# An encoder layer's first twenty microseconds: constants loaded late, transposes in three pairs of banks, four weight loads issued from ScalarE

## The chip, the cores and the metric

The kernel runs on one core of a Trainium2 chip. The metric is the device time of the whole kernel in microseconds (us), lower is better. A core has five engines that run side by side, each through its own instruction stream in order: TensorE (PE, matmuls and transposes), VectorE (DVE), ScalarE (ACT), GpSimd (POOL) and SyncE (SP). SyncE and ScalarE can issue transfers (DMAs) from memory into the core; an engine that issues one does nothing else until the issue instruction is over. Engines meet only through semaphores.

## What is computed

One layer of an encoder over 512 tokens of width 1024, in float32, in three sub-layers. Each normalizes its input, works, normalizes the result and adds it to the residual:

```python
h = swiglu(rmsnorm(x, ffn1_pre_norm), ffn1_w_gate, ffn1_w_up, ffn1_w_down)   # 1024 -> 2816 -> 1024
x = x + 0.5 * rmsnorm(h, ffn1_post_norm)
h = hybrid_mixer(rmsnorm(x, mix_pre_norm), w_in, ..., w_out)                 # attention and a gated recurrence
x = x + rmsnorm(h, mix_post_norm)
h = swiglu(rmsnorm(x, ffn2_pre_norm), ffn2_w_gate, ffn2_w_up, ffn2_w_down)
x = x + 0.5 * rmsnorm(h, ffn2_post_norm)

def swiglu(x, w_gate, w_up, w_down):
    return (silu(x @ w_gate) * (x @ w_up)) @ w_down
```

The change touches only what happens before and during the first few matmuls of the first `swiglu`, and four small constants (`hgrn_lb_fwd`, `hgrn_lb_bwd`, `hgrn_out_norm`, `attn_sink`) that are not needed before the mixer, hundreds of microseconds later.

## The kernel before

**Split operands.** Every product of the layer's matrices is made from three matmuls: each operand is split into a high part (rounded to the type `float32r`) and a low part (what is left). For activations these are `XH` and `XL`, for weights `WH` and `WL`. The three matmuls of lines 832 to 834 are `WH`·`XH`, `WH`·`XL` and `WL`·`XH`.

**Weights.** They come in units of 128 x 1024 elements (512 KB). A unit passes through one of four slots: SyncE issues the load into `raw` (line 334), ScalarE makes `WH` by a rounding copy (`hi`, line 492), GpSimd makes `WL` by a subtraction (`lo`, line 413), and TensorE uses them. For the first feed-forward the units alternate between `w_gate` and `w_up`; a unit of gate or up is loaded as 1024 rows of 512 bytes. `ahead(n)` in ScalarE's stream means "make `WH` up to unit n". The first four units are numbers 0 to 3.

**Activations.** The tokens stand in four chunks `c` of 128. For a chunk, ScalarE squares and sums `X[c]` (`square_x`, line 514) and takes the root (`rms_x`, line 539), VectorE takes the reciprocal and writes the normalized chunk to `YB` in two halves (`normed`, lines 1280 and 1286), TensorE transposes it, four 128 x 128 blocks to a half, into a bank of PSUM (`turn`, line 857), ScalarE copies the bank to `XH` (`split_high`, line 546) and VectorE subtracts to get `XL` (`split_low`, line 1295). PSUM has eight banks, `ps[0]` to `ps[7]`. The row of pre-norm weights is spread over all partitions by two matmuls (line 944) into `ps[6]` and `ps[7]`.

**Order at the beginning.** Each engine's order is the order in which its block is written. SyncE issues the identity matrix (needed by every transpose), then `X[0]`, `X[1]`, unit 0, `X[2]`, unit 1, `X[3]`, units 2 and 3. ScalarE issues five small transfers first, the row of norm weights and the four constants, and then starts on `X`. TensorE turns the constants (`vec_rows`, 17 rows) into columns before the first chunk is turned (line 947), and VectorE copies them out (line 1324) before it normalizes the first chunk. All four chunks are turned through the same two banks, `ps[4]` and `ps[5]`, so each chunk waits until `XL` of the chunk before is done.

**First units.** `first_units` runs the first four units twice, each time for half of the tokens (`part` 0 and 1, 256 columns, 24 matmuls for a unit and part): part 0 needs only chunks 0 and 1. Chunk 2 is turned ahead of unit 0, chunk 3 between unit 0 and unit 1. After that a loop runs two gate and two up units a turn, and TensorE, ScalarE, VectorE and GpSimd follow one another through it.

Of the kernel before, what the change touches and what calls it, by code (L numbers as in the profile page):

```python
# [5 lines left out]
P = 128  # L6
# [3 lines left out]
KD = D // P  # L10
# [5 lines left out]
NH = 4  # L16
# [5 lines left out]
NSLOT = 4  # L22
# [95 lines left out]
def encoder_layer(nc, io, out):  # L118
# [3 lines left out]
    with ctx:  # L122
# [155 lines left out]
        def y_bank(s, c, h):  # L278


            return ps[(4, 2, 6, 4)[c] + h] if s == 2 else ps[(0 if h else 4) + c]
# [8 lines left out]
            return 8 * s + 2 * c + h + 1  # L290

        def turn_bank(s, c, h):
            return y_bank(s, c, h) if s else ps[4 + h]


        def wait_y(e, s, c, h):
# [30 lines left out]
        def _(sp):  # L327
            def load(n, quarter, src):

                if n >= NSLOT:  # L330
                    sp.wait_ge(lo_done, quarter * NSLOT + (n - NSLOT + 1))
                nk = src.shape[1]
                dst = raw[:, n % NSLOT, 0:nk * src.shape[2]].rearrange("p (k f) -> p k f", k=nk)
                sp.dma_start(dst, src).then_inc(raw_full[n % NSLOT], 16)
# [9 lines left out]
            def load_x(c):  # L344
                sp.dma_start(X[:, c, :], io["x"][0, chunk(c), :]).then_inc(x_in[c], 16)

            def norm_weights(to, name):
                sp.dma_start(to[:, :, :], io[name][0].partition_broadcast(P).rearrange("p (h f) -> p h f", h=2)).then_inc(weights_in, 16)

            def load_ffn(s, first):  # L350
                gate, up, down = w_of[s]
                for b in range(NSLOT):
                    load(first + b, 0, (gate, up)[b % 2][:, :, (b // 2) * P:(b // 2 + 1) * P])
                    if s == 1 and b < 2:
                        load_x(2 + b)
                with sp.Fori(0, KF // 2 - 1) as i:
                    for b in range(NSLOT):
                        load(first + NSLOT + b, i, (gate, up)[b % 2][:, :, bass.ds(i * (2 * P) + (2 + b // 2) * P, P)])
                for h in range(2):
                    for u in range(KP):  # L360
                        load(first + N_UP + KP * h + u, 0, down[:, 2 * u:2 * u + 2, h * TOK:(h + 1) * TOK])
                        if (h, u) == (0, KP - 1):
                            sp.wait_ge(h_ready, KF * s)
                            norm_weights(TMP, f"ffn{s}_post_norm")
                            if s == 1:
                                norm_weights(SQ, "mix_pre_norm")

            sp.dma_start(ident[:, :], io["t_square"][:, 0:P]).then_inc(ident_in, 16)
            load_x(0)
            load_x(1)  # L370
            load_ffn(1, FFN1)
            for u, unit in enumerate(MIXU):
                if u == NSLOT:
# [104 lines left out]
        def _(act):  # L478
# [92 lines left out]
                    square_y(2 * f + 1, c, 0)  # L571
                ahead(first + N_UP + N_DOWN - 1)

            row = 0
            act.dma_start(TMP[0:1, :, :], io["ffn1_pre_norm"].rearrange("o (h f) -> o h f", h=2)).then_inc(row_in, 16)
            for name in ("hgrn_lb_fwd", "hgrn_lb_bwd"):
                act.dma_start(vec_rows[row:row + 2 * NH, :], io[name].rearrange("r (h p) -> (r h) p", p=P)).then_inc(const_in, 16)
                row += 2 * NH
            act.dma_start(sink[:, :], io["attn_sink"][0].partition_broadcast(P)).then_inc(const_in, 16)
            act.dma_start(vec_rows[4 * NH:NV, :], io["hgrn_out_norm"]).then_inc(const_in, 16)  # L580
            act.wait_ge(set_up, 1)
            preload(ACT.Sqrt)
            for c in range(2):
# [1 line left out]
                rms_x(0, c)  # L585
            ahead(0)
            split_high(0, 0)
            square_x(0, 2)
            rms_x(0, 2)
            ahead(1)  # L590
            split_high(0, 1)
            square_x(0, 3)
            rms_x(0, 3)
            split_high(0, 2)
            ahead(2)
            split_high(0, 3)
            ahead(3)
            act.wait_ge(lb_max, 1)
            nc.scalar.activation(lbr, lbr, ACT.Exp).then_inc(lb_exp, 1)
            ffn(0, FFN1)  # L600
# [227 lines left out]
        def _(pe):  # L828
# [14 lines left out]
            def turn(s, c):  # L843

                for h in range(2):
                    bank = turn_bank(s, c, h)
                    pe.wait_ge(xhat_ready, half_count(s, c, h))
                    if s == 1:
                        pe.wait_ge(x_ready, half_count(0, c, 1))
                        pe.wait_ge(squared, square_count("y", 1, 1, c))  # L850
                    elif s == 2:
                        pe.wait_ge(x_ready, half_count(1, c, 1))
                        pe.wait_ge(squared, square_count("y", 2, 1, c))
                    elif c:
                        pe.wait_ge(xl_ready, half_count(s, c - 1, h))
                    for j in range(4):
                        mm = nc.tensor.transpose(bank[:, j * P:(j + 1) * P], YB[:, 4 * h + j, chunk(c)], ident[:, :])  # L857
                    mm.then_inc(x_turned, 1)
# [17 lines left out]
            def first_units(f, first):  # L876


                s = 2 * f
                turn(s, 2)  # L880
                for part in range(2):
                    t = slice(part * 2 * P, (part + 1) * 2 * P)
                    for u in range(NSLOT):
                        if not u:
                            pe.wait_ge(xl_ready, half_count(s, 2 * part + 1, 1))
                        if not part:
                            pe.wait_ge(lo_done, first + u + 1)
                            if f and not u:
                                pe.wait_ge(mixl_a, TT)
                        for k in range(KD):  # L890
                            mm = three(ps[u][:, t], (first + u) % NSLOT, k, XH[:, k, t], XL[:, k, t], not k, k == KD - 1)
                        if part:
                            mm.then_inc(unit_used, 1)
                        elif u == f:
                            turn(s, 3)

            def ffn(f, first):

# [38 lines left out]
                if not f:  # L937
                    turn(1, 2)

            pe.wait_ge(ident_in, 16)  # L940
            pe.wait_ge(row_in, 16)
            pe.wait_ge(set_up, 1)
            for h in range(2):
                mm = nc.tensor.matmul(ps[6 + h][:, :], SQ[0:1, 0, 0:P], TMP[0:1, h, :], start=True, stop=True)
            mm.then_inc(row_spread, 1)
            pe.wait_ge(const_in, CONST_IN)
            nc.tensor.transpose(ps[4][:, 0:NV], vec_rows[:, :], ident[0:NV, 0:NV]).then_inc(vecs_turned, 1)
            pe.wait_ge(vecs_taken, 1)
            turn(0, 0)
            turn(0, 1)  # L950
            ffn(0, FFN1)
# [286 lines left out]
        def _(dve):  # L1238
# [81 lines left out]
            nc.vector.memset(ones[:, :], 1.0)  # L1320
            nc.vector.memset(eps[:, :], EPS)
            nc.vector.memset(SQ[0:1, 0, 0:P], 1.0).then_inc(set_up, 1)
            dve.wait_ge(vecs_turned, 1)
            nc.vector.tensor_copy(vecs[:, :], ps[4][:, 0:NV]).then_inc(vecs_taken, 1)
            dve.wait_ge(row_spread, 1)
            normed(0, 0)
            normed(0, 1)
            split_low(0, 0)
            normed(0, 2)
            split_low(0, 1)  # L1330
            normed(0, 3)
            split_low(0, 2)
            split_low(0, 3)
            dve.wait_ge(vecs_taken, 1)
            dve.wait_ge(const_in, CONST_IN)
            nc.vector.tensor_scalar(sink_less[:, :], sink[:, :], -1.0, None, ALU.mult)
# [330 lines left out]
```

## Time and profile before

| | |
|---|---|
| time, median of 3 runs | 1064.55 us (1064.37 to 1065.12) |
| the profiled execution's own time | 1064.92 us |
| its span in the profile | 1063.1 us |
| PE busy | 1046.3 us, 98% |
| DVE, ACT, POOL busy | 425.2, 363.4 and 450.5 us |
| mean granted TensorE clock | 0.999 of full speed |

The span runs from the first to the last instruction that the profiler saw; 1.8 us lie around it. TensorE is busy nearly all the time, so what counts is when its stream of matmuls begins, what else it has to execute, and where it waits.

### The profile page before, as it was taken

The page shows a single profiled execution, that of the slowest core. Times are in us where ns is not written, and L with a number is a line of the kernel's source. Part 1 is how long each engine was busy: PE and PEld are TensorE (multiplying, and loading weights), DVE is VectorE, ACT ScalarE, POOL GpSimd, SP SyncE. Part 2 cuts the span into 40 slices and gives each one's busy share as a digit, 9 for nine tenths or more (in the row PEclk, how much of TensorE's full clock was granted, in tenths as well). Part 3 has the DMA queues.
Part 4 walks back from the last instruction along what each step waited for, and adds up shares of the span by engine and source line. Part 5 has one row for each costly group of instructions (what it writes and reads, how often), then busy time and mean ns, then how long its engine had stood idle before and what let it go on. Part 6 is the DMA issues. An engine that isn't in the chain of part 4 may idle for free.

```text
span 1063.1 us, 13360 instructions
## 1 busy us (share of the span) xinstructions
PE 1046.3 (98%) x5075; PEld 866.8 (82%) x5075; DVE 425.2 (40%) x621; ACT 363.4 (34%) x540; POOL 450.5 (42%) x299
## 2 busy tenths in 40 slices
PE   6999999999999999999999999999999999999997
PEld 5988888888888878888777878898888888888886
DVE  4443443434001160365757576644434343420103
ACT  6322222222112264513656575542222222221211
POOL 3444444444444246863324134135444444444440
PEclk9999999999999999999999999999999999999999
DMA  6333333323433243332010114024323333333212
GB/s 221 99 99 99 99 99 89 99 89 99 138 99 99 80 137 100 80 99 60 21 40 21 41 40 139 10 74 136 99 86 98 92 99 99 99 99 119 98 41 80
DMA packets 136300, 96.00 MB, mean 90 GB/s; under 512 B 11442, under 2 KB 120387, under 8 KB 136260
## 3 DMA queue, kind: packets, MB, share of 16 engines
q1 hardware_dynamic: 136080, 95.43, 29.8%
q8 instruction: 27, 0.44, 0.2%
q14 instruction: 13, 0.11, 0.0%
q10 hardware_dynamic: 180, 0.02, 0.0%
HBM read 93.34 MB, written 2.10 MB: 90 GB/s over the span
## 4 chain that ended last, share of the span: by engine, by line
PE 94%; DVE 3%; ACT 1%; issue 1%; DMA 1%; ACTq 0%; DVEq 0%
PE ps L832 19%; PE ps L834 18%; PE ps L833 18%; PE ps L841 9%; PE ps L840 9%; PE ps L839 9%; PE ps L998 2%; PE ps L1092 2%; PE ps L1032 1%; PE ps L1115 1%; PE ps L857 1%; PE ps L1102 1%; DVE YB L1286 1%; ACT SQX L514 1%; DMA vec_rows<-hgrn_out_norm 1%
## 5 line engine op out<-in xcount | busy, mean ns | idle before, releaser
L413 POOL TENSOR_TENSOR WL<-raw,WH 128x1024 fp32r<-128x1024 f32 x132 | 317.1, 2404 | 424.3 <-ACT WH L492 424.3
L832 PE MATMUL ps<-XH,WH 128*128 128x512 f32 (+1 forms) x944 | 360.8, 382 | 0.1
L834 PE MATMUL ps<-XH,WL 128*128 128x512 f32 (+1 forms) x944 | 354.7, 376 | 0.0
L833 PE MATMUL ps<-XL,WH 128*128 128x512 f32 (+1 forms) x944 | 354.5, 376 | 0.0
L492 ACT ACTIVATE WH<-raw 128x1024 fp32r<-128x1024 f32 x162 | 171.0, 1056 | 324.9 <-PE ps L834 172.5
L832 PEld LDWEIGHTS ps<-XH,WH 128*128 128x128 f32 x944 | 178.4, 189 | 44.4 <-issue 13.7
L834 PEld LDWEIGHTS ps<-XH,WL 128*128 128x128 f32 x944 | 178.2, 189 | 32.5
L833 PEld LDWEIGHTS ps<-XL,WH 128*128 128x128 f32 x944 | 178.4, 189 | 31.9 <-issue 1.2
L839 PE MATMUL ps<-WH,hh 128*128 128x512 f32 x352 | 137.1, 389 | 0.0
L841 PE MATMUL ps<-WL,hh 128*128 128x512 f32 x352 | 137.0, 389 | 0.0
L430 POOL TENSOR_TENSOR WL<-raw,WH 128x256 fp32r<-128x256 f32 x120 | 95.2, 828 | 98.5 <-ACT WH L492 98.3
L840 PE MATMUL ps<-WH,hl 128*128 128x512 f32 x352 | 136.9, 389 | 0.0
L1314 DVE TENSOR_TENSOR hl<-SQ,hh 128x512 f32 x44 | 118.7, 2697 | 5.4
L1310 DVE TENSOR_TENSOR SQ<-ps,TMP 128x512 f32<-128x512 f32 x44 | 30.4, 692 | 169.7 <-PE ps L834 169.7
L1256 DVE TENSOR_TENSOR ps<-ps,TMP 128x512 f32<-128x512 f32 x16 | 11.2, 698 | 204.7 <-ACT SQX L514 204.5
L556 ACT ACTIVATE SQX<-ps 128x512 f32<-128x512 f32 x44 | 26.3, 598 | 190.9 <-PE ps L834 190.9
L840 PEld LDWEIGHTS ps<-WH,hl 128*128 128x128 f32 x352 | 66.1, 188 | 13.8
L839 PEld LDWEIGHTS ps<-WH,hh 128*128 128x128 f32 x352 | 66.1, 188 | 13.7
L841 PEld LDWEIGHTS ps<-WL,hh 128*128 128x128 f32 x352 | 66.1, 188 | 13.6
L1307 DVE TENSOR_TENSOR TMP<-ps,SQX 128x512 f32<-128x512 f32 x44 | 30.4, 691 | 94.1 <-ACT SQX L556 94.1
L440 POOL TENSOR_TENSOR W<-Qh,Fg 128x512 f32<-128x512 f32 x8 | 10.3, 1290 | 52.4 <-ACT Fg L666 52.4
L998 PE MATMUL ps<-W,KM 128*128 128x128 f32 x224 | 30.7, 279 | 0.7 <-ACT KM L656 0.7
(163 smaller groups left out, 881.3 us busy)
## 6 DMA issues: line engine op xcount, KB each, us to landing
raw<-ffn_w_gate SPq DMA_DIRECT2D x44, 512.0 KB, 3.7
raw<-ffn_w_up SPq DMA_DIRECT2D x44, 512.0 KB, 3.7
raw<-ffn_w_down SPq DMA_DIRECT2D x44, 512.0 KB, 3.7
raw<-w_in SPq DMA_DIRECT2D x22, 512.0 KB, 3.7
raw<-w_out SPq DMA_DIRECT2D x8, 512.0 KB, 3.3
X<-x SPq DMA_DIRECT2D x4, 512.0 KB, 6.5
raw<-w_in SPq DMA_DIRECT2D x8, 256.0 KB, 3.2
out<-X SPq DMA_DIRECT2D x8, 256.0 KB, 2.0
```

The lines of the kernel that those rows point to most:

```text
L413: pool.tensor_tensor(low, raw[:, s, :], high.bitcast(fp32), ALU.subtract).then_inc(lo_done, 1)
L430: ins = pool.tensor_tensor(WL[:, s, f], raw[:, s, f], WH[:, s, f].bitcast(fp32), ALU.subtract)
L492: nc.scalar.activation(to, raw[:, s, :], ACT.Copy).then_inc(hi_done, 1)
L832: nc.tensor.matmul(dst, WH[:, s, w], xh, start=first, stop=False)
L833: nc.tensor.matmul(dst, WH[:, s, w], xl, start=False, stop=False)
L834: return nc.tensor.matmul(dst, WL[:, s, w], xh, start=False, stop=last)
L839: nc.tensor.matmul(dst, xh, wh, start=first, stop=False)
L840: nc.tensor.matmul(dst, xl, wh, start=False, stop=False)
L841: return nc.tensor.matmul(dst, xh, wl, start=False, stop=last)
L998: mm = nc.tensor.matmul(sides[:, c], KM[:, (g - 1) % 2, chunk(c)], level_queries(h, g - 1, c), start=True, stop=True)
L1307: nc.vector.tensor_tensor(TMP[:, a, :], ps[2 * a][:, :], SQX[:, a, :], ALU.mult).then_inc(gate_taken, 1)
L1314: nc.vector.tensor_tensor(hl[:, j, :], SQ[:, a, :], hh[:, j, :].bitcast(fp32), ALU.subtract).then_inc(h_ready, 1)
```

## The change

ScalarE now issues only the row of norm weights and then the loads of units 0 to 3. SyncE issues `X[0]`, `X[1]`, the identity, `X[2]`, `X[3]`, and after them the four constants. TensorE turns chunks 0 and 1 right away, chunk 2 between units 1 and 2, chunk 3 between units 2 and 3, and the constants at the head of part 1. The chunks are turned through three pairs of banks (`4,5`, `2,3`, `4,5`, `6,7`), so that only chunk 2 still waits for an earlier chunk's `XL`. ScalarE copies chunks 0 and 1 in one go before it makes `WH` of unit 1; VectorE subtracts chunks 0 and 1 before it normalizes chunk 2.

```diff
--- before.py
+++ after.py
@@ -290,7 +290,7 @@
             return 8 * s + 2 * c + h + 1
 
         def turn_bank(s, c, h):
-            return y_bank(s, c, h) if s else ps[4 + h]
+            return y_bank(s, c, h) if s else ps[(4, 2, 4, 6)[c] + h]
 
 
         def wait_y(e, s, c, h):
@@ -347,12 +347,24 @@
             def norm_weights(to, name):
                 sp.dma_start(to[:, :, :], io[name][0].partition_broadcast(P).rearrange("p (h f) -> p h f", h=2)).then_inc(weights_in, 16)
 
+            def load_constants():
+
+                row = 0
+                for name in ("hgrn_lb_fwd", "hgrn_lb_bwd"):
+                    sp.dma_start(vec_rows[row:row + 2 * NH, :], io[name].rearrange("r (h p) -> (r h) p", p=P)).then_inc(const_in, 16)
+                    row += 2 * NH
+                sp.dma_start(vec_rows[4 * NH:NV, :], io["hgrn_out_norm"]).then_inc(const_in, 16)
+                sp.dma_start(sink[:, :], io["attn_sink"][0].partition_broadcast(P)).then_inc(const_in, 16)
+
             def load_ffn(s, first):
                 gate, up, down = w_of[s]
-                for b in range(NSLOT):
-                    load(first + b, 0, (gate, up)[b % 2][:, :, (b // 2) * P:(b // 2 + 1) * P])
-                    if s == 1 and b < 2:
-                        load_x(2 + b)
+                if s == 1:
+                    load_x(2)
+                    load_x(3)
+                    load_constants()
+                else:
+                    for b in range(NSLOT):
+                        load(first + b, 0, (gate, up)[b % 2][:, :, (b // 2) * P:(b // 2 + 1) * P])
                 with sp.Fori(0, KF // 2 - 1) as i:
                     for b in range(NSLOT):
                         load(first + NSLOT + b, i, (gate, up)[b % 2][:, :, bass.ds(i * (2 * P) + (2 + b // 2) * P, P)])
@@ -365,9 +377,9 @@
                             if s == 1:
                                 norm_weights(SQ, "mix_pre_norm")
 
-            sp.dma_start(ident[:, :], io["t_square"][:, 0:P]).then_inc(ident_in, 16)
             load_x(0)
             load_x(1)
+            sp.dma_start(ident[:, :], io["t_square"][:, 0:P]).then_inc(ident_in, 16)
             load_ffn(1, FFN1)
             for u, unit in enumerate(MIXU):
                 if u == NSLOT:
@@ -571,13 +583,10 @@
                     square_y(2 * f + 1, c, 0)
                 ahead(first + N_UP + N_DOWN - 1)
 
-            row = 0
             act.dma_start(TMP[0:1, :, :], io["ffn1_pre_norm"].rearrange("o (h f) -> o h f", h=2)).then_inc(row_in, 16)
-            for name in ("hgrn_lb_fwd", "hgrn_lb_bwd"):
-                act.dma_start(vec_rows[row:row + 2 * NH, :], io[name].rearrange("r (h p) -> (r h) p", p=P)).then_inc(const_in, 16)
-                row += 2 * NH
-            act.dma_start(sink[:, :], io["attn_sink"][0].partition_broadcast(P)).then_inc(const_in, 16)
-            act.dma_start(vec_rows[4 * NH:NV, :], io["hgrn_out_norm"]).then_inc(const_in, 16)
+            for b in range(NSLOT):
+                src = w_of[1][b % 2][:, :, (b // 2) * P:(b // 2 + 1) * P]
+                act.dma_start(raw[:, b, :].rearrange("p (k f) -> p k f", k=KD), src).then_inc(raw_full[b], 16)
             act.wait_ge(set_up, 1)
             preload(ACT.Sqrt)
             for c in range(2):
@@ -585,16 +594,16 @@
                 rms_x(0, c)
             ahead(0)
             split_high(0, 0)
+            split_high(0, 1)
+            ahead(1)
             square_x(0, 2)
             rms_x(0, 2)
-            ahead(1)
-            split_high(0, 1)
+            ahead(2)
             square_x(0, 3)
             rms_x(0, 3)
+            ahead(3)
             split_high(0, 2)
-            ahead(2)
             split_high(0, 3)
-            ahead(3)
             act.wait_ge(lb_max, 1)
             nc.scalar.activation(lbr, lbr, ACT.Exp).then_inc(lb_exp, 1)
             ffn(0, FFN1)
@@ -851,8 +860,8 @@
                     elif s == 2:
                         pe.wait_ge(x_ready, half_count(1, c, 1))
                         pe.wait_ge(squared, square_count("y", 2, 1, c))
-                    elif c:
-                        pe.wait_ge(xl_ready, half_count(s, c - 1, h))
+                    elif c == 2:
+                        pe.wait_ge(xl_ready, half_count(0, 0, h))
                     for j in range(4):
                         mm = nc.tensor.transpose(bank[:, j * P:(j + 1) * P], YB[:, 4 * h + j, chunk(c)], ident[:, :])
                     mm.then_inc(x_turned, 1)
@@ -877,12 +886,16 @@
 
 
                 s = 2 * f
-                turn(s, 2)
+                if f:
+                    turn(s, 2)
                 for part in range(2):
                     t = slice(part * 2 * P, (part + 1) * 2 * P)
                     for u in range(NSLOT):
                         if not u:
                             pe.wait_ge(xl_ready, half_count(s, 2 * part + 1, 1))
+                            if part and not f:
+                                pe.wait_ge(const_in, CONST_IN)
+                                nc.tensor.transpose(ps[4][:, 0:NV], vec_rows[:, :], ident[0:NV, 0:NV]).then_inc(vecs_turned, 1)
                         if not part:
                             pe.wait_ge(lo_done, first + u + 1)
                             if f and not u:
@@ -891,8 +904,10 @@
                             mm = three(ps[u][:, t], (first + u) % NSLOT, k, XH[:, k, t], XL[:, k, t], not k, k == KD - 1)
                         if part:
                             mm.then_inc(unit_used, 1)
-                        elif u == f:
+                        elif f and u == 1:
                             turn(s, 3)
+                        elif not f and u in (1, 2):
+                            turn(s, 1 + u)
 
             def ffn(f, first):
 
@@ -937,15 +952,12 @@
                 if not f:
                     turn(1, 2)
 
-            pe.wait_ge(ident_in, 16)
             pe.wait_ge(row_in, 16)
             pe.wait_ge(set_up, 1)
             for h in range(2):
                 mm = nc.tensor.matmul(ps[6 + h][:, :], SQ[0:1, 0, 0:P], TMP[0:1, h, :], start=True, stop=True)
             mm.then_inc(row_spread, 1)
-            pe.wait_ge(const_in, CONST_IN)
-            nc.tensor.transpose(ps[4][:, 0:NV], vec_rows[:, :], ident[0:NV, 0:NV]).then_inc(vecs_turned, 1)
-            pe.wait_ge(vecs_taken, 1)
+            pe.wait_ge(ident_in, 16)
             turn(0, 0)
             turn(0, 1)
             ffn(0, FFN1)
@@ -1320,17 +1332,17 @@
             nc.vector.memset(ones[:, :], 1.0)
             nc.vector.memset(eps[:, :], EPS)
             nc.vector.memset(SQ[0:1, 0, 0:P], 1.0).then_inc(set_up, 1)
-            dve.wait_ge(vecs_turned, 1)
-            nc.vector.tensor_copy(vecs[:, :], ps[4][:, 0:NV]).then_inc(vecs_taken, 1)
             dve.wait_ge(row_spread, 1)
             normed(0, 0)
             normed(0, 1)
             split_low(0, 0)
+            split_low(0, 1)
             normed(0, 2)
-            split_low(0, 1)
             normed(0, 3)
             split_low(0, 2)
             split_low(0, 3)
+            dve.wait_ge(vecs_turned, 1)
+            nc.vector.tensor_copy(vecs[:, :], ps[4][:, 0:NV]).then_inc(vecs_taken, 1)
             dve.wait_ge(vecs_taken, 1)
             dve.wait_ge(const_in, CONST_IN)
             nc.vector.tensor_scalar(sink_less[:, :], sink[:, :], -1.0, None, ALU.mult)
```

ScalarE's stream at its beginning, before (names as above; `raw_full0` is the arrival of unit 0, `x_in0` that of `X[0]`):

```order
L575 DMA TMP<-ffn_pre_norm 1x1024
L577 DMA vec_rows<-hgrn_lb_fwd 8x128
L577 DMA vec_rows<-hgrn_lb_bwd 8x128
L579 DMA sink<-attn_sink 128x8
L580 DMA vec_rows<-hgrn_out_norm 1x128
L506 ACT_TABLE_LOAD
L506 ACTIVATE small<-eps 128x1 [waits set_up]
L514 ACTIVATE SQX,stats<-X 128x1024 [waits x_in0]
L539 ACTIVATE stats<-stats,eps 128x1 [waits squared]
```

The same place now:

```order
L586 DMA TMP<-ffn_pre_norm 1x1024
L589 DMA raw<-ffn_w_gate 128x8x128
L589 DMA raw<-ffn_w_up 128x8x128
L589 DMA raw<-ffn_w_gate 128x8x128
L589 DMA raw<-ffn_w_up 128x8x128
L518 ACT_TABLE_LOAD
L518 ACTIVATE small<-eps 128x1 [waits set_up]
L526 ACTIVATE SQX,stats<-X 128x1024 [waits x_in0]
L551 ACTIVATE stats<-stats,eps 128x1 [waits squared]
```

Four small transfers have left ScalarE's stream, and four of 512 KB stand ahead of the table load and the first square.

TensorE's stream from its beginning to the first matmuls of unit 0, before (`ident,YB` are the transposes, eight to a chunk):

```order
L944 MATMUL ps<-TMP,SQ 128x512 x2
L947 MATMUL ps<-ident,vec_rows 128x17
L857 MATMUL ps<-ident,YB 128x128 x24
L832 MATMUL ps<-XH,WH 128x256
L833 MATMUL ps<-XL,WH 128x256
L834 MATMUL ps<-XH,WL 128x256
```

And now, with the place between units 1 and 2 and the one between units 2 and 3:

```order
L958 MATMUL ps<-TMP,SQ 128x512 x2
L866 MATMUL ps<-ident,YB 128x128 x16
...
L866 MATMUL ps<-ident,YB 128x128 x8
L841 MATMUL ps<-XH,WH 128x256
...
L866 MATMUL ps<-ident,YB 128x128 x8
...
L898 MATMUL ps<-ident,vec_rows 128x17
```

Eight transposes (chunk 2) and the turn of the constants have moved from ahead of the first matmul to behind it.

## Rows read from the trace of the kernel before

**Rows 1.** The page's chain that ended last, shares of the span by engine.

```profile
PE 94%; DVE 3%; ACT 1%; issue 1%; DMA 1%; ACTq 0%; DVEq 0%
```

**Rows 2.** Waits of PE after 18.2 us: total, times, longest (us); the longest.

```profile
PE ps L857 <- DVE YB L1286: 0.9, 2, 0.5
```

**Rows 3.** Timeline of ScalarE: start us, us, instruction, [idle before <-releaser].

```profile
2.69 1.28 ACT L506 ACT_TABLE_LOAD   x1 [2.69 <-issue]
5.12 1.06 ACT L514 ACTIVATE SQX<-X 128x1024 f32<-128x1024 f32 x1 [0.94 <-DMA X<-x]
6.30 0.29 ACT L539 ACTIVATE stats<-stats,eps 128x1 f32<-128x1 f32 x1
6.50 1.04 ACT L514 ACTIVATE SQX<-X 128x1024 f32<-128x1024 f32 x1
...
9.75 1.06 ACT L492 ACTIVATE WH<-raw 128x1024 fp32r<-128x1024 f32 x1 [1.79 <-DMA raw<-ffn_w_gate]
11.30 0.60 ACT L546 ACTIVATE XH<-ps 128x512 fp32r<-128x512 f32 x1 [0.49 <-PE ps L857]
```

**Rows 4.** Waits in the first 12 us: the constants.

```profile
PEld ps L947 <- DMA vec_rows<-hgrn_out_norm: 3.8, 1, 3.8
```

**Rows 5.** Timeline of VectorE, 9 to 14 us.

```profile
9.09 0.15 DVE L1280 RECIPROCAL stats<-stats 128x1 f32<-128x1 f32 x1
9.29 1.40 DVE L1286 SCALAR_TENSOR_TENSOR YB<-X,stats,ps 128x512 f32<-128x512 f32 x2
...
10.80 1.40 DVE L1286 SCALAR_TENSOR_TENSOR YB<-X,stats,ps 128x512 f32<-128x512 f32 x2
12.12 1.35 DVE L1295 TENSOR_TENSOR XL<-ps,XH 128x512 fp32r<-128x512 f32 x2
```

**Rows 6.** Timeline of TensorE, 10 to 23 us.

```profile
10.18 1.94 PE L857 MATMUL ps<-ident,YB 128*128 128x128 f32 x8 [1.21 <-DVE YB L1286]
...
16.50 1.94 PE L857 MATMUL ps<-ident,YB 128*128 128x128 f32 x8 [1.61 <-DVE XL L1295]
...
18.09 0.56 PE L832 MATMUL ps<-XH,WH 128*128 128x256 f32 x1
...
22.25 1.04 PE L857 MATMUL ps<-ident,YB 128*128 128x128 f32 x8
```

**Rows 7.** Stretches: length, PE and PEld busy (x instructions), ...; the last numbers are granted clock, DMA share and GB/s.

```profile
18.00:20.70 2.70, 2.70 (x15) 2.70 (x14) 2.23 (x4) 1.76 (x3) 0.61 (x1) 1.00 0.65 191
20.70:31.60 10.90, 10.90 (x93) 10.90 (x93) 4.60 (x10) 5.02 (x7) 4.19 (x2) 1.00 0.33 99
```

**Rows 8.** Timeline of GpSimd: `WL` of unit 0.

```profile
10.89 2.37 POOL L413 TENSOR_TENSOR WL<-raw,WH 128x1024 fp32r<-128x1024 f32 x1 [10.44 <-ACT WH L492]
```

**Rows 9.** Timeline of SyncE's queue: start us, us that the issue took.

```profile
2.20 0.43 SPq L334 DMA_DIRECT2D raw<-ffn_w_gate  x1
2.68 0.58 SPq L345 DMA_DIRECT2D X<-x  x1
3.30 0.48 SPq L334 DMA_DIRECT2D raw<-ffn_w_up  x1
3.82 4.55 SPq L345 DMA_DIRECT2D X<-x  x1
...
8.90 2.15 SPq L334 DMA_DIRECT2D raw<-ffn_w_up  x1
```

**Rows 10.** DMA issues by window: KB each, us to landing; units 0 and 1.

```profile
DMA to landing us min/median/max: 7.5/7.5/7.5
...
raw<-ffn_w_up SPq DMA_DIRECT2D x1, 512.0 KB, 9.2
```

**Rows 11.** Line 334 near 385 us: durations ns, starts; landing; then its next two.

```profile
L334 SPq DMA_DIRECT2D raw<-w_in x2: 432/508/585, 384.9 to 385.4; - x2
...
DMA to landing us min/median/max: 8.0/8.6/9.1
...
L334 SPq DMA_DIRECT2D raw<-w_in x2: 1112/2200/3289, 388.1 to 391.8; - x2
```

**Rows 12.** DMA traffic, 0 to 12 us in 40 slices of 0.3 us.

```profile
GB/s 0 0 0 0 0 26 157 173 109 205 316 355 302 420 328 423 396 369 126 56 2 36 51 85 119 235 306 370 352 393 457 423 394 369 333 326 355 382 408 428
```

## The prediction, made before the change was run

> **What bounds the kernel now.** I read the chain that ended last first: 94% of it is TensorE [rows 1]. Then its waits after 18.2 us: the longest group is 0.9 us in all [rows 2]. So from its first real matmul, at 18.09 us [rows 6], TensorE works without a stop to the end, and the time is the start of that stream plus its length. A microsecond off the start is a microsecond off the kernel, and so is one put on. The profiled span is 1063.1 us in a run of 1064.92; the median is 0.37 us below that run. I add a difference in span straight to the median.
>
> Next, what made the start 18.09. ScalarE's first square began at 5.12, when `X[0]` had landed [rows 3]. Roots were ready soon after (6.30 + 0.29), but TensorE stood 3.8 us for the last constant to land [rows 4], so VectorE took its first reciprocal only at 9.09 [rows 5]. Then the chunks went through one pair of banks: chunk 2's transposes had to wait 1.61 us for `XL` [rows 6], began at 16.50 and, eight in 1.94 us, held up the first matmul. The rebuilt order removes both, the constants' wait and chunk 2's turn, from the path.
>
> **What the change makes of ScalarE.** Call T the moment when ScalarE has issued its fourth weight load. All that follows hangs on T, since table load, squares and roots stand behind it in the same stream. The chain from T, from rows:
> - Table load 1.28 and the little activation behind it: square of chunk 0 starts at T+1.5. From square to root's start 6.30-5.12 = 1.2, root 0.3: root of chunk 0 at T+3.0. Second square 1.4 after the first (6.50-5.12), so the second root ends at T+4.4 [rows 3].
> - VectorE: first reciprocal T+3.05. Before, reciprocal at 9.09, `YB` of chunk 0 at 9.29, of chunk 1 at 10.80 [rows 5], TensorE's eight transposes from 10.18 for 1.94 [rows 6]. Counted from the reciprocal: chunk 0 turned from +1.1 to +3.0; chunk 1's second half of `YB` is there at +3.1, its turn follows without a wait and ends at +5.0, at the same pace.
> - ScalarE copies the last half (0.60 [rows 3]) until +5.65, VectorE subtracts (0.68, half of 1.35 [rows 5]) until +6.35. First matmul at +6.45, which is **T+9.5**.
> - Does unit 0 keep up? Its `WH` is made from T+4.3 to T+5.3 (1.06 [rows 3]), `WL` takes 2.37 [rows 8] until T+7.8. Yes. Unit 1's `WH` comes behind the copies, T+8.7 to T+9.75, `WL` until T+12.2; unit 0's 24 matmuls last some 4 us (2.70 for the first 15, then 0.117 each [rows 7]), until about T+13.5. Units 2 and 3: `WL` at T+14.6 and T+17.1, wanted at T+17.3 and T+20.2 (24 matmuls x 0.12 = 2.9 a unit, 0.9 for a turn). All hidden, with 1.3, 2.7 and 3.1 us to spare. Were one cover gone, its lateness would come on top one for one.
> - The constants' turn, at the head of part 1, costs 0.15 us of TensorE; their transfers have had 20 us to land. ScalarE's exponential waits for them, with two table loads around it, some 3 us beyond the head of part 1; its first gate activation is due 2.9 us beyond, and TensorE asks for its product only after four units, 11.6 us. Hidden.
>
> **What TensorE gets to do behind its first matmul.** Chunk 2's turn is now inside the stream, at the price of chunk 3's there, 1.04 less the overlap at its end: 0.9 us [rows 6]. Constants 0.15. Clock: the granted clock reads 1.00 throughout, but 15 instructions took the first 2.70 us and 93 the next 10.90 [rows 7], 0.18 against 0.117 us each: the first stretch went partly at the lower of the two levels (1.2 GHz against 2.4). Before that TensorE had turned chunks 1 and 2. Now it has a 1.5 us pause between chunk 1's turn and unit 0. I bound the slow stretch at no longer and 1.5 us longer: 0 to 0.5 us, taken as 0.3. Sum: **change = (T + 9.5 - 18.09) + 0.9 + 0.15 + 0.3 = T - 7.2.** Break-even is T = 7.2 us.
>
> **How large is T?** An issue without resistance takes 0.43 to 0.58 us on SyncE's queue [rows 9], and four behind the row would end near 3.1. But SyncE did not get through: with units 0 and 1 issued, `X[3]` was held for 4.55 us, to 8.37, and unit 3 for 2.15 us, to 11.05 [rows 9]. Landings: unit 0 at 2.20 + 7.5 = 9.7, unit 1 at 3.30 + 9.2 = 12.5 [rows 10]. So unit 3 was let in 1.45 us before unit 1 landed. The same pile stands at 385 us: two weight units issued at 384.9 and 385.4 landed at 392.9 and 394.5; the third, tried at 388.1, was in after 3.29 us at 391.4, the fourth, from 391.8 for 1.11, at 392.9 [rows 11]: each 1.5 to 1.6 us before the one two places ahead of it landed. My reading: a queue takes two such units, and a third when the first is almost over. I see this on SyncE's queue only; ScalarE's small issues were never held. If its queue is the same, ScalarE is held at unit 2 and again at unit 3, and **T is about unit 1's landing less 1.5**.
>
> Unit 1 landed at 12.5 behind the identity, `X[0]`, `X[1]`, unit 0 and `X[2]`. Now it is issued at about 1.8, ahead of `X[2]`: one 512 KB transfer less, at some 380 GB/s [rows 12] 1.4 us, gives 11.1 and T = 9.6. That holds if transfers of both queues go in order of issue. If instead `X[2]` and `X[3]`, on the other queue, take their share before unit 1 ends, it lands at 13.9 and T = 12.4. The slump from 5.4 to 7.2 us [rows 12], in which little moved, may go with the small constants out of the way: up to 1.5 us off, T = 8.1. I take T = 10.3, a change of 10.3 - 7.2 = +3.1 us.
>
> The order across queues is where the Trainium skill speaks (DMA: Bandwidth & Descriptors, Queues, rings and completion order): an engine of the DMA hardware takes turns between the queues that have work for it, a packet at a time. By that rule `X[2]` and `X[3]` would share with the weights, and T would be near the upper of the two values, a change of about +5. The constant's late landing speaks rather for order of issue, so the sum stays with its own value.
>
> **Rivals.**
> 1. *ScalarE is not held* (ends faster). Each issue costs 0.43 to 0.58 us and T is 3.1. `X[0]` is issued 0.4 earlier than before and lands at about 4.7 (5.12 less 0.4 [rows 3]), which is as if T were 3.2; the later gate is unit 0, whose `WH` stands ahead of the copies: landed at about 9.7 as before, `WH` to 10.8, four copies at 0.53 to 0.60 to 13.0, `XL` 13.7, first matmul 13.8. Change: 13.8 - 18.09 + 1.35 = -2.9, time 1061.6. It decides when T is below 5.1. For it: five issues on ScalarE's queue were over by 2.69 [rows 3], unhindered. Against: they were of 4 KB and less, and the hold shows at two places wherever a third unit is asked for. Chance 0.15. The Trainium skill states it this way (the same page, Issuing engines are not separate DMA queues): issuing from several engines saves only the sequencer's time, usually small beside the transfer. It names no hold; the rows show one, on SyncE.
> 2. *Only unit 3 is held, and until unit 0 is nearly in*: the limit is three units, as `X[3]`'s release 1.3 us ahead of unit 0's landing could be read. Unit 0 is behind 1 MB of `X` only and lands at 8.5 to 9.7, so T = 7.2 to 8.4, or up to 9.3 with some sharing. Change 0 to +2.1, time about 1065.3. Against: unit 3 and the fourth at 385 us waited longer than this. Chance 0.22.
> 3. *Held as forecast*, T 9.3 to 12.5: +2.1 to +5.3, time 1067.6. Chance 0.57.
> 4. *Worse*: both queues share, and `WL` of a late unit or a longer slow stretch adds: beyond 1069.9. Chance 0.06.
>
> **How the numbers follow.** No change can be told from one of about 0.2%, 2.1 us. Faster is rival 1: 0.15. Slower is cases 3 and 4: 0.63. The rest, 0.22, is rival 2. The likeliest time is 1064.55 + 3.1 = 1067.6; its own range is 1066.6 to 1069.9. The 8-in-10 range runs from 1063.8, which leaves out most of rival 1, to 1070.2.
>
> **What would show it.** Step by step in the new profile: on ScalarE's queue two weight issues of about 0.45 us, then one or two of several microseconds; table load starting near 10 and not at 3; `X[0]` landed long before its square; no wait of TensorE on the constants; first matmul about 9.5 us behind the table load's start, near 20; eight transposes of 0.9 us between units 1 and 2; no new wait later. I am wrong if the issues on ScalarE's queue are all short, if unit 1 lands before 9, or if TensorE waits on `WL` of units 1 to 3.

## The result, and the profile after

| | |
|---|---|
| changed kernel, median of 11 runs | 1067.56 us (1066.6 to 1070.06) |
| kernel before, median of 11 runs | 1064.78 us (1064.32 to 1066.0) |
| ratio | 1.003, 95% interval 1.0021 to 1.0039 |
| profiled execution: its time, its span | 1069.64 us, 1067.8 us |

The change made the kernel slower by 2.8 us, 0.3%. The profiled execution lies 2.1 us above its median, that of before 0.1 us above its own; the two traces therefore differ by more, 4.7 us of span, and a part of that difference needs an explanation of its own.

The chain that ended last is still TensorE's, but the constants' transfer (the 1% of DMA in [rows 1]) has gone from it and ScalarE's issues have come in (ACTq stands for ScalarE's queue):

```profile
PE 93%; DVE 3%; ACT 2%; ACTq 1%; issue 1%; DVEq 0%
```

ScalarE's timeline (start us, us, instruction), the place of [rows 3]:

```profile
1.31 0.41 ACTq L589 DMA_DIRECT2D raw<-ffn_w_gate  x1
1.75 0.59 ACTq L589 DMA_DIRECT2D raw<-ffn_w_up  x1
2.38 4.74 ACTq L589 DMA_DIRECT2D raw<-ffn_w_gate  x1
7.14 4.51 ACTq L589 DMA_DIRECT2D raw<-ffn_w_up  x1
11.69 1.28 ACT L518 ACT_TABLE_LOAD   x1 [11.69 <-issue]
...
13.09 1.04 ACT L526 ACTIVATE SQX<-X 128x1024 f32<-128x1024 f32 x1
...
15.82 1.04 ACT L504 ACTIVATE WH<-raw 128x1024 fp32r<-128x1024 f32 x1
```

Two issues of about half a microsecond, then two of 4.74 and 4.51 us. Nothing else of ScalarE's stream ran meanwhile: the table load starts at 11.69 instead of 2.69, the first square at 13.09 instead of 5.12, without a wait for `X[0]`, which had long landed. T, the moment at which ScalarE is free, is 11.69.

The landings of this kernel's transfers, from its issues by window (KB each, us from issue to landing): units 0 and 1, and `X[3]`, issued at about 2.6:

```profile
raw<-ffn_w_gate ACTq DMA_DIRECT2D x1, 512.0 KB, 10.3
raw<-ffn_w_up ACTq DMA_DIRECT2D x1, 512.0 KB, 11.4
...
X<-x SPq DMA_DIRECT2D x1, 512.0 KB, 7.7
```

Unit 0 landed at 11.6 and unit 1 at 13.15, `X[3]` before both, at 10.3, though it was issued after them. T is 1.5 us ahead of unit 1's landing, as unit 3's issue was in [rows 9, 10] and the fourth in [rows 11]. Unit 2, though, was let in at 7.12, 4.5 us ahead of unit 0's landing.

TensorE's timeline, the place of [rows 6]:

```profile
15.75 3.65 PE L866 MATMUL ps<-ident,YB 128*128 128x128 f32 x16 [9.44 <-DVE YB L1298]
20.81 0.58 PE L841 MATMUL ps<-XH,WH 128*128 128x256 f32 x1 [1.41 <-DVE XL L1307]
...
25.03 0.39 PE L842 MATMUL ps<-XL,WH 128*128 128x256 f32 x1
25.24 0.30 PE L843 MATMUL ps<-XH,WL 128*128 128x256 f32 x1
...
28.62 1.03 PE L866 MATMUL ps<-ident,YB 128*128 128x128 f32 x8
...
36.19 0.23 PE L898 MATMUL ps<-ident,vec_rows 17*128 17x17 f32 x1
```

Chunks 0 and 1 are turned back to back through two pairs of banks, but 5.6 us later than chunk 0 was. The first matmul runs at 20.81, not 18.09. 20 matmuls are slow: up to 25.24 they follow one another by 0.21 us (the first by 0.38), from there by 0.12. Before, 12 were slow, up to 20.80. Chunk 2's turn now stands inside the stream, at 28.62. After it TensorE waits nowhere that it did not wait before: the longest groups of its waits behind the start of the stream are

```profile
PE ps L841 <- DVE XL L1307: 1.4, 1, 1.4
PE ps L866 <- DVE YB L1298: 0.9, 2, 0.5
```

of which the first is the wait ahead of the first matmul itself and the second is that of [rows 2]. The slump in the traffic of [rows 12] is no longer at 5.4 to 7.2 us, but it has moved rather than gone. In the same slices of 0.3 us a shorter one stands at 9.3 to 11.4 us:

```profile
GB/s 0 0 0 0 0 68 191 123 341 410 328 423 341 382 437 393 251 270 316 335 367 382 389 401 425 389 413 393 442 387 366 304 162 111 89 103 180 277 345 341
```

From 9 to 11 us the packets (the pieces in which a transfer moves) were these:

```profile
DMA packets 594, 0.37 MB, mean 186 GB/s; under 512 B 156, under 2 KB 554, under 8 KB 594
```

156 of them were under 512 bytes, against 35 from 6 to 9 us. The only transfer in such small rows is that of the constant `sink` (128 rows of 32 bytes), which SyncE had issued with the others behind `X[3]`, by 4.6 us. So this slump, with the constants in it, lay ahead of the landings of units 0 and 1. What it cost was not tried by itself.

### The profile page after: what moved, and what is told of

Same layout as the page of the kernel before. It is cut to its first block, busy times and chain, and to the rows that moved or that the text cites. A ratio compares the mean times of both kernels' runs of the same rounds, so it can differ in the third digit from the quotient of the medians.

```text
span 1067.8 us, 13357 instructions
## 1 busy us (share of the span) xinstructions
PE 1046.2 (98%) x5075; PEld 867.0 (81%) x5075; DVE 423.5 (40%) x621; ACT 363.3 (34%) x540; POOL 450.1 (42%) x299
## 4 chain that ended last, share of the span: by engine, by line
PE 93%; DVE 3%; ACT 2%; ACTq 1%; issue 1%; DVEq 0%
PE ps L841 19%; PE ps L842 18%; PE ps L843 18%; PE ps L850 9%; PE ps L848 9%; PE ps L849 9%; PE ps L1010 2%; PE ps L1104 2%; PE ps L1044 1%; PE ps L1127 1%; ACTq L589 1%; PE ps L866 1%; PE ps L1114 1%; ACT SQX L526 1%; PE ps L1021 1%
## 5 line engine op out<-in xcount | busy, mean ns | idle before, releaser
L452 POOL TENSOR_TENSOR W<-Qh,Fg 128x512 f32<-128x512 f32 x8 | 10.3, 1290 | 52.5 <-ACT Fg L675 52.5
```

## The experiments

Each ratio is to the kernel before, run on the same chip; its median was 1064.7 to 1065.0 us in these runs. Theory A: ScalarE is held by its own issues, and that alone turns a gain into a loss.

**1. The weight loads back on SyncE's queue, all the rest rebuilt.** The constants thereby come behind the four units.

```diff
# ScalarE
-            for b in range(NSLOT):
-                act.dma_start(raw[:, b, :]..., src).then_inc(raw_full[b], 16)
# SyncE, behind X[0], X[1] and the identity
+                for b in range(NSLOT):
+                    load(first + b, 0, ...)
+                    if s == 1 and b < 2:
+                        load_x(2 + b)
+                if s == 1:
+                    load_constants()
```

> The rebuilt beginning with the four weight loads back on SyncE's queue, in the order of before (X0, X1, identity, unit 0, X2, unit 1, X3, units 2 and 3, constants). Theory A, ScalarE is held by its own issues and the rest of the rebuild gains: ScalarE is free at about 1.3 us, squares X0 at 4.7, unit 0 lands at 8.2 to 9.7, first matmul at 13.2 to 14.7 instead of 20.81; about 1062.3 us, 2 to 3 us below the kernel before. Theory B, the hold is incidental and the loss is the work that was moved behind the first matmul (chunk 2's turn, constants) and a longer slow stretch of the clock: still 1.7 us or more above before, about 1066.5.

Measured: 1060.85 us (5 runs, 1058.9 to 1061.86), ratio 0.9956 (0.9942 to 0.997). Its timelines of ScalarE and TensorE:

```profile
1.30 1.28 ACT L517 ACT_TABLE_LOAD   x1 [1.30 <-PEq L1667]
...
4.13 1.06 ACT L525 ACTIVATE SQX<-X 128x1024 f32<-128x1024 f32 x1 [1.34 <-DMA X<-x]
...
7.58 1.06 ACT L503 ACTIVATE WH<-raw 128x1024 fp32r<-128x1024 f32 x1 [0.56 <-DMA raw<-ffn_w_gate]
```

```profile
12.53 0.58 PE L837 MATMUL ps<-XH,WH 128*128 128x256 f32 x1 [1.41 <-DVE XL L1303]
```

ScalarE is free at 1.30, the first square waits only for `X[0]`, the first matmul stands at 12.53. Theory A holds and theory B falls: against the changed kernel this edit is worth 6.7 us by the medians. It did better than expected, because unit 0 had landed by 7.58 and not at 8.2 to 9.7; experiment 6 is on that.

**2 and 3. Two and three of the four units issued by ScalarE**, the others by SyncE behind `X[3]`.

```diff
-            for b in range(NSLOT):
+            for b in range(2):        # experiment 3: range(3)
                 act.dma_start(raw[:, b, :]..., src).then_inc(raw_full[b], 16)
# SyncE, behind load_x(3)
+                    for b in range(2, NSLOT):
+                        load(first + b, 0, ...)
```

> As the changed kernel, but ScalarE issues units 0 and 1 only; SyncE issues units 2 and 3 behind X3. Theory A: no hold, ScalarE free at 2.4 us. But the weights share the DMA engines with X, and unit 0 landed only at 11.6 in the changed kernel; if it does here too, its high part is made at 11.6 to 12.7, ahead of the copies of chunk 0 in ScalarE's order, first matmul near 15.9; about 1064.3 us. If the holds were about the total in flight and not about one queue, ScalarE is still held for several us, first matmul 19 to 21, 1067 us.

> ScalarE issues units 0 to 2, SyncE unit 3. Theory A (a queue takes two such units and a third when the first is almost over): ScalarE is held once, until about 7.1 us; unit 0 lands near 11.6 all the same, so the first matmul is near 16 and the time near 1064.4 us, like the kernel with two. The rival, a limit by the total in flight: held into 11 us as in the changed kernel, 1067.5 us.

Measured: 1063.41 us (11 runs), ratio 0.9987 (0.9978 to 0.9996), and 1063.34 us (10 runs), ratio 0.9989 (0.9979 to 0.9998). ScalarE with two units, then TensorE's first matmul there:

```profile
2.37 1.28 ACT L520 ACT_TABLE_LOAD   x1 [2.37 <-issue]
...
10.96 1.06 ACT L506 ACTIVATE WH<-raw 128x1024 fp32r<-128x1024 f32 x1 [3.77 <-DMA raw<-ffn_w_gate]
```

```profile
15.08 0.58 PE L843 MATMUL ps<-XH,WH 128*128 128x256 f32 x1 [3.70 <-DVE XL L1309]
```

And with three:

```profile
2.37 4.72 ACTq L591 DMA_DIRECT2D raw<-ffn_w_gate  x1
7.12 1.28 ACT L520 ACT_TABLE_LOAD   x1 [7.12 <-issue]
...
11.26 1.04 ACT L506 ACTIVATE WH<-raw 128x1024 fp32r<-128x1024 f32 x1
```

```profile
16.24 0.39 PE L843 MATMUL ps<-XH,WH 128*128 128x256 f32 x1 [1.41 <-DVE XL L1309]
16.46 0.28 PE L844 MATMUL ps<-XL,WH 128*128 128x256 f32 x1
```

The rival of both expectations, a limit by the total in flight, had ScalarE held into 11 us; it was free at 2.37 and at 7.12. The first hold comes with the third unit. It puts the first matmul 1.2 us later (16.24 against 15.08), yet with T at 2.37 or at 7.12 the medians are the same. With two units the copies of chunk 0 wait for unit 0, landed at 10.9, because its `WH` stands ahead of them; with three, T + 9.1 (the chain as measured in the changed kernel, 20.81 - 11.69) is 16.2, just beyond. In the profiled runs the later start was made up by the clock: with three units only one matmul was slow, against 20 with two. Whether that holds for the other runs is not known. These runs show two prices apart. Handing units 0 and 1 to a second queue beside `X` delays unit 0 by 3.4 us (10.96 against 7.58), which costs some 2.5 us; the second hold, from 7.1 to 11.7, costs 4.2 more. The queues are not independent, though. SyncE was held too, in experiment 2 at its second weight unit and in experiment 3 at the first constant, a transfer of 8 rows:

```profile
3.66 2.39 SPq L334 DMA_DIRECT2D raw<-ffn_w_up  x1
```

```profile
3.75 2.47 SPq L354 DMA_DIRECT2D vec_rows<-hgrn_lb_fwd  x1
```

By then SyncE's queue had been given 1664 rows in experiment 3 (the identity and four chunks of `X`, 128 rows each, and one unit of 1024). In the kernel before it took 2560 rows (the identity, three chunks, units 0 and 1) with no issue over 0.6 us [rows 9]. So the other queue's transfers count in some way.

**4. The kernel before, with nothing changed but the issues of the weights.** SyncE's four loads are taken out (not shown).

```diff
             act.dma_start(vec_rows[4 * NH:NV, :], io["hgrn_out_norm"]).then_inc(const_in, 16)
+            for b in range(NSLOT):
+                act.dma_start(raw[:, b, :]..., src).then_inc(raw_full[b], 16)
```

> The kernel before with nothing changed but that ScalarE issues the four weight loads, behind the row and the four constants. Theory A: ScalarE free at about 12.5 us, then the old chain through one pair of banks, 12 us from there to the first matmul: 24.5 us instead of 18.09, about 1071 us. Theory B (the hold costs little): within 1 us of before.

Measured: 1071.29 us (4 runs, 1070.44 to 1071.48), ratio 1.0059 (1.0043 to 1.0074). ScalarE:

```profile
4.08 6.61 ACTq L585 DMA_DIRECT2D raw<-ffn_w_gate  x1
10.71 2.24 ACTq L585 DMA_DIRECT2D raw<-ffn_w_up  x1
12.99 1.28 ACT L508 ACT_TABLE_LOAD   x1 [12.99 <-issue]
```

The part that harms does so alone, and by the size worked out. In the same kernel SyncE issued its four transfers of `X`, 512 KB each in 128 rows, without a hold:

```profile
1.19 1.92 SPq L345 DMA_DIRECT2D X<-x  x4
```

**5. The same bytes in longer rows.** The four units are taken from `w_down`, so the first four units' products are with other weights than the layer's and the result is wrong; only the time is of use.

```diff
-                src = w_of[1][b % 2][:, :, (b // 2) * P:(b // 2 + 1) * P]
-                act.dma_start(raw[:, b, :].rearrange("p (k f) -> p k f", k=KD), src)...
+                src = w_of[1][2][:, 2 * b:2 * b + 2, 0:TOK]
+                act.dma_start(raw[:, b, :].rearrange("p (k f) -> p k f", k=2), src)...
```

> As the changed kernel, but the four units that ScalarE issues are taken from w_down, the same 512 KB each in 256 rows of 2 KB instead of 1024 rows of 512 bytes (so the first four units multiply with other weights than the layer's). Theory, the limit of a queue is in rows: nothing is held, ScalarE is free at 3.1 us, first matmul 13 to 14.5 us, about 1061.5 to 1063. Rival, the limit is in bytes or in number of transfers: held into 11 us as before, 1067.5 us.

Measured: 1060.13 us (5 runs), ratio 0.9958 (0.9944 to 0.9971). ScalarE:

```profile
1.31 2.06 ACTq L589 DMA_DIRECT2D raw<-ffn_w_down  x4
3.40 1.28 ACT L518 ACT_TABLE_LOAD   x1 [3.40 <-issue]
...
8.33 1.06 ACT L504 ACTIVATE WH<-raw 128x1024 fp32r<-128x1024 f32 x1 [0.70 <-DMA raw<-ffn_w_down]
```

Four issues in 2.06 us. Number of transfers and bytes are those of the changed kernel; the rows went from 1024 to 256 a unit (and the tensor read is another). So the hold goes by rows. Unit 0 also landed 3.3 us earlier, at 8.3; the last issue was over at 3.4, so it was not an earlier landing that let the four in.

**6. The constants' transfers first, in experiment 1's kernel.**

```diff
             act.dma_start(TMP[0:1, :, :], ...).then_inc(row_in, 16)
+            for name in ("hgrn_lb_fwd", "hgrn_lb_bwd"):
+                act.dma_start(vec_rows[row:row + 2 * NH, :], ...).then_inc(const_in, 16)
+            act.dma_start(sink[:, :], ...).then_inc(const_in, 16)
+            act.dma_start(vec_rows[4 * NH:NV, :], ...).then_inc(const_in, 16)
```

> As the first experiment (weights on SyncE, late turn of the constants), but ScalarE issues the four constants behind the row as in the kernel before; nobody needs them early. Theory, their small transfers bring the slump in the traffic between 5.4 and 7.2 us: it comes back, unit 0 lands at 9.5 and not at 7.6, first matmul near 14.5, 1062.8 us. Rival, the slump came from the order on SyncE's queue: no slump, 1060.9 us.

Measured: 1062.99 us (9 runs, 1061.63 to 1063.92), ratio 0.9977 (0.9966 to 0.9988). Traffic and the arrival of unit 0:

```profile
GB/s 0 0 0 0 0 55 273 123 423 396 369 280 362 410 343 336 261 81 38 32 44 46 64 89 178 243 272 367 401 405 369 387 413 353 358 360 358 387 418 405
```

```profile
10.10 1.06 ACT L501 ACTIVATE WH<-raw 128x1024 fp32r<-128x1024 f32 x1 [2.92 <-DMA raw<-ffn_w_gate]
```

The slump is back, from 5.1 to 7.2 us, and unit 0 lands 2.5 us later. So the constants, 13 KB in all, cost by being transferred early on ScalarE's queue, whether or not anybody waits for them: some 2 us by the medians.

**7 and 8. The two useful parts of the rebuild, each alone on the kernel before**, the weights on SyncE in both: late constants, and the pairs of banks with the new order. Of each edit only the core is shown; in 7 SyncE also issues the constants behind unit 3 and VectorE copies them out late, in 8 the turns and the orders of ScalarE and VectorE are the changed kernel's.

```diff
# 7
-            pe.wait_ge(const_in, CONST_IN)
-            nc.tensor.transpose(ps[4][:, 0:NV], vec_rows[:, :], ...).then_inc(vecs_turned, 1)
-            pe.wait_ge(vecs_taken, 1)
             turn(0, 0)
+                            if part and not f:      # in first_units
+                                pe.wait_ge(const_in, CONST_IN)
+                                nc.tensor.transpose(ps[4][:, 0:NV], vec_rows[:, :], ...).then_inc(vecs_turned, 1)
# 8
-            return y_bank(s, c, h) if s else ps[4 + h]
+            return y_bank(s, c, h) if s else ps[(4, 2, 4, 6)[c] + h]
```

> The kernel before with the constants late and nothing else: they are issued by SyncE behind unit 3 and turned at the head of part 1; one pair of banks, old order of turns and units. ScalarE is free at 1.3 us, squares X0 near 4.7, VectorE's reciprocal near 6.2, then the old chain of 9.0 us from there to the first matmul, 15.2 to 15.7 instead of 18.09: about 1062.2 us (-2.5 against before). If the two parts of the rebuild only pay together, less than 1 us.

> The kernel before with the three pairs of banks and the new order of turns and units alone; constants loaded and turned first as before, weights from SyncE. VectorE's reciprocal stays near 9.1, the first matmul follows 6.15 us behind it, near 15.2, but chunk 2's turn (0.9 us) is inside the stream and the slow stretch may be 1.7 us longer (0.7 to 0.8 us of loss): about 1063.7 us (-1.2). The rival, that the parts are worth nothing one by one, expects 1065.

Measured: 7: 1062.87 us (11 runs, 1062.07 to 1066.07), ratio 0.999 (0.9981 to 0.9999). 8: 1061.61 us (7 runs, 1061.12 to 1063.7), ratio 0.9973 (0.9962 to 0.9984). Both parts pay alone; by medians -1.8 and -3.1 us, together (experiment 1) -4.15. The first is barely clear of the noise: its interval ends at 0.9999, and its ratio stands for 1.1 us only. In experiment 7 the first matmul stood at 16.18, half a microsecond beyond the expected 15.2 to 15.7, since `WH` of unit 0 ended at 9.9 and pushed chunk 0's copies back. Its first matmul:

```profile
16.18 0.56 PE L837 MATMUL ps<-XH,WH 128*128 128x256 f32 x1
```

In experiment 8 it stood where expected, and its profiled run was the slowest of its seven:

```profile
15.34 0.58 PE L841 MATMUL ps<-XH,WH 128*128 128x256 f32 x1 [1.41 <-DVE XL L1307]
```

19 slow matmuls followed it. That run took 1063.7 us, as the expectation had it; the median lies 2.1 us below.

**9. The changed kernel once more.**

> The changed kernel unaltered, one more look. Its runs spread over 3.5 us (1066.6 to 1070.1), those of before over 1.7. Theory A: the start varies little (issue over at 11.4 to 12.0 us), and what varies is the slow stretch of TensorE's clock behind the first matmul, 20 slow matmuls in the profiled run of 1069.6 and 1 in the third experiment's; with few of them here the run takes near 1067.3. Rival: the moment at which ScalarE's issues are over varies by 2 to 3 us from run to run.

Measured: 1068.69 us. ScalarE was free at 11.40, 0.3 us earlier than in the first profile:

```profile
11.40 1.28 ACT L518 ACT_TABLE_LOAD   x1 [11.40 <-issue]
```

The last of its slow matmuls:

```profile
23.46 0.32 PE L842 MATMUL ps<-XL,WH 128*128 128x256 f32 x1
```

14 matmuls were slow, six fewer, at 0.21 - 0.12 us each 0.55. The two add to 0.85, the times differ by 0.95. Between these two runs the holds vary little and the slow stretch differs more, though 14 is not the few that the expected 1067.3 needed. Two runs don't settle what varies over all of them.

**10. TensorE kept busy, in experiment 1's kernel.**

```diff
             pe.wait_ge(ident_in, 16)
+            for j in range(3):
+                nc.tensor.transpose(ps[0][:, j * P:(j + 1) * P], ident[:, :], ident[:, :])
             turn(0, 0)
             turn(0, 1)
+            for j in range(5):
+                nc.tensor.transpose(ps[j // 4][:, j % 4 * P:(j % 4 + 1) * P], ident[:, :], ident[:, :])
```

> As the first experiment (weights on SyncE), with idle TensorE made to work: three extra transposes of the identity ahead of chunk 0's turn and five between chunk 1's turn and unit 0, into banks that the units overwrite later. Theory: the slow stretch (19 matmuls of 0.21 instead of 0.12 us in the first experiment) ends earlier relative to the first matmul, up to 1.8 us gained, 1059.1 us. Rival: the clock's rise does not depend on this, 1060.9, or up to 0.5 more because the extra transposes are in the way.

Measured: 1059.04 us (5 runs, 1058.88 to 1059.37), ratio 0.9949 (0.9935 to 0.9962). TensorE:

```profile
6.28 0.90 PE L958 MATMUL ps<-ident 128*128 128x128 f32 x3
7.38 3.29 PE L862 MATMUL ps<-ident,YB 128*128 128x128 f32 x16 [0.21 <-DVE YB L1298]
10.51 0.71 PE L962 MATMUL ps<-ident 128*128 128x128 f32 x5
12.22 0.38 PE L837 MATMUL ps<-XH,WH 128*128 128x256 f32 x1 [1.00 <-DVE XL L1307]
12.44 0.28 PE L838 MATMUL ps<-XL,WH 128*128 128x256 f32 x1
```

The second matmul is already a fast one, where experiment 1's kernel had 19 slow. But the five extra transposes behind the turns can't have done it. They took 0.71 us together, where the three ahead of the turns took 0.90: TensorE was fast before they began, having sped up inside the turns (16 transposes in 3.29 us, 3.65 in the changed kernel), and 1.00 us behind them stayed idle. And experiment 5's kernel, which has no extra transposes, did the same:

```profile
8.37 3.42 PE L866 MATMUL ps<-ident,YB 128*128 128x128 f32 x16 [1.93 <-DMA ident<-t_square]
13.21 0.39 PE L841 MATMUL ps<-XH,WH 128*128 128x256 f32 x1 [1.41 <-DVE XL L1307]
13.43 0.28 PE L842 MATMUL ps<-XL,WH 128*128 128x256 f32 x1
```

The runs lie within 0.5 us, those of experiment 1 within 3.0, but two of those five took 1058.9 and 1059.1 without any extra transpose, and the intervals of the two ratios overlap. That the three transposes ahead of the turns make the early rise more certain is likely and not shown. This is the fastest version found, 5.7 us below before.

## Why the prediction came out right, step by step

- **The bound** was read rightly. From one profile to the other the first matmul moved by 2.7 us, and what follows it grew by 2.0: chunk 2's turn 0.9, eight more slow matmuls 0.75, the constants 0.15, and 0.2 that I did not place. Together this is the 4.7 us of span, and no wait arose later.
- **The hold** was the right mechanism and in the right place. The rule that sets T, the fourth unit let in 1.5 us before the second lands, was met in all nine profiles in which one queue issued the four units in rows of 512 bytes (1.4 to 1.5 us). It is no rule for two queues: in experiment 2 the last unit was in at 6.05, 7.9 us ahead of unit 1's landing. For the third unit on ScalarE's queue it failed, without a consequence for T: it got in at 7.1, 4.5 us ahead of unit 0's landing. Why the third gets in so much earlier is open. Experiments 1, 4 and 5 show that the hold decides the sign. Experiment 5, with T at 3.4, is what rival 1 describes; with rows of 512 bytes it was wrong. Rival 2 was wrong too: unit 2 was held as well, and unit 3 until 11.65, when unit 0 was in.
- **T** was sized too low: 11.69 and 11.40 measured, 10.3 taken. The step that went wrong is the choice between order of issue and a share for `X[2]` and `X[3]`. I gave weight to the constant's late landing; the trace has `X[3]` landed at 10.3, ahead of unit 0, which had been issued 1.3 us before it. The Trainium skill's rule (DMA: Bandwidth & Descriptors, Queues, rings and completion order), turns between queues packet by packet, agrees with this trace, where `X`, on the other queue, moves in rows of 4 KB and the weights in rows of 512 bytes. By it T came out at 12.4. The prediction's other term, the slump, had shrunk and not gone: in the two traffic lines about 1.9 us of traffic are missing before (against 380 GB/s) and about 1.0 now (against 350), an estimate. That would take most of a microsecond off 12.4, which is argued and not tested.
- **The chain from T** was 9.1 us and not 9.5.
- **The clock** was priced at 0.3 us, with 0.5 as the upper end; between the two profiles it was 0.75. A range from a single trace was too narrow: 1 to 23 matmuls were slow in the profiles of this study.
- **The sum**, T - 7.2, gives +4.5 with the measured T, and the profiled run has 4.7. The median is +2.8. That 1067.6 was forecast and 1067.56 measured is thus partly luck: T too low, and a median run that lies 2.1 us below the profiled one. Experiments 9 and 10 make the slow stretch the likely reason for the latter, which is argued and not shown, since only profiled runs can be counted.

## What to carry to other kernels

Before moving a transfer to a compute engine's queue, look at how long such issues took where they stood, the longest and not the median, and count the rows of what is in flight: the engine's whole stream stands behind a held issue. Load what is needed late, late, even a few KB, and behind the urgent loads of the other queue too. And where a stream of matmuls bounds the kernel, look at the distance of its first matmuls in several runs: up to 2 us lay there. Work for an idle TensorE ahead of the stream is worth a try.

## What the runs showed of the hardware

- The hold goes by rows, not by bytes or by number of transfers: 4 x 512 KB in 1024 rows each took 10.3 us to issue, in 256 rows 2.06 us, in 128 rows 1.92 us. A small transfer is held as well: one of 8 rows for 2.47 us in experiment 3. The two queues share some of it, since SyncE's had been given 1664 rows then and took 2560 in the kernel before; what they share is open.
- Four transfers with 13 KB together, on the second queue, left the DMA engines nearly idle for about 2 us (32 to 89 GB/s against some 380) and delayed a 512 KB transfer by 2.5 us. Behind `X[3]` on SyncE's queue they went with a shorter slump, down to 89 GB/s, in the changed kernel, and with none in experiments 2 and 5 (131 and 129 packets under 512 bytes within 12 to 14 and 9 to 12 us, at 319 and 405 GB/s). Which of the four does it was not tried.
- The granted clock reads 1.00 in all these rows; the slow stretch shows only in the distance between matmuls, 0.21 and 0.12 us at 256 columns, which goes with the levels of 1.2 and 2.4 GHz. In the changed kernel TensorE had stood idle for 9.4 us until the turns and 1.4 us behind them, and it rose 4.4 us after the first matmul. In experiment 10, with extra transposes and 1.0 us of the second gap left idle, it rose inside the turns, ahead of the first matmul. In experiments 3 and 5 it rose ahead of the first matmul too, with the gap of 1.4 us as it was, so a gap does not settle it in every run. The same code gave 20 slow matmuls in one profile and 14 in another.
